# Row numbers and gathers of experts 1 and 2 moved ahead of the first expert's products in a mixture-of-experts decoder step

## What is computed

```python
logits = x @ w_router + b_router
top_v, top_e = lax.top_k(logits, 4)
gates = jax.nn.softmax(top_v, axis=-1)
# for each expert e, over the rows of the tokens that chose it:
h = xb @ w_gate_up[e] + b_gate_up[e]
gate = jnp.minimum(h[:, 0::2], 7.0)
up = jnp.clip(h[:, 1::2], -7.0, 7.0)
out = ((up + 1.0) * gate * jax.nn.sigmoid(gate * 1.702)) @ w_down[e] + b_down[e]
# y = h_in + sum over the four chosen experts of gate * out, then RMSNorm
```

## Time and profile before

| | us |
|---|---|
| median of three runs | 1385.93 |
| the profiled execution | 1385.96 |
| its span, first to last instruction | 1384.1 |
| TensorE busy (matmul) | 1352.9 |
| VectorE busy | 1209.8 |
| ScalarE busy | 1091.7 |
| GpSimd busy | 1010.1 |
| weights moved, with all else | 458.99 MB, mean 332 GB/s |

### The profile page before, as it was taken

One profiled execution on the slowest core, in us unless ns is written; L12 is line 12 of the kernel. 1 busy time (PEld: TensorE's weight loads), 2 busy tenths in 40 slices (PEclk: granted clock), 3 DMA queues, 4 the chain that ended last, 5 costly groups with the idle time before them and its releaser, 6 DMA issues.

```text
span 1384.1 us, 19701 instructions
## 1 busy us (share of the span) xinstructions
PE 1352.9 (98%) x6762; PEld 994.0 (72%) x6762; DVE 1209.8 (87%) x1092; ACT 1091.7 (79%) x1149; POOL 1010.1 (73%) x431
## 2 busy tenths in 40 slices
PE   8999999999999999999999999999999999999995
PEld 5988655667777777777777777777777777777773
DVE  5466556899999999999999999999999999999996
ACT  5354423778888888888888888888888888888885
POOL 2122211266699999899999998999999989999943
PEclk9999999999999999999999999999999999999998
DMA  9522272999999999999999999999999999999984
GB/s 354 189 66 72 88 276 70 367 394 356 372 351 377 378 369 382 372 392 379 377 393 373 378 382 375 379 384 365 389 380 365 381 390 374 382 371 386 375 313 150
DMA packets 51803, 458.99 MB, mean 332 GB/s; under 512 B 11450, under 2 KB 15516, under 8 KB 26122
## 3 DMA queue, kind: packets, MB, share of 16 engines
q1 hardware_dynamic: 40089, 438.33, 80.9%
q0 software_dynamic: 10000, 18.19, 6.0%
q10 hardware_dynamic: 1648, 1.65, 0.4%
HBM read 446.62 MB, written 22.08 MB: 339 GB/s over the span
## 4 chain that ended last, share of the span: by engine, by line
PE 77%; DMA 3%; DVE 1%; issue 1%; POOL 1%; ACT 0%; POOLq 0%; ACTq 0%; DVEq 0%
PE psum L2371 24%; PE psum L2373 24%; PE psum L2372 24%; DMA area<-hn_tbl,idx_i 3%; PE psum L2355 2%; PE psum L2366 2%; POOL small L810 0%; DVE low L1690 0%; PE psum L2342 0%; DVE area L1812 0%; POOL area L695 0%; DVE area L1772 0%; DVE ring L1836 0%; DVE area L1765 0%; POOL out L820 0%
## 5 line engine op out<-in xcount | busy, mean ns | idle before, releaser
L1690 DVE TENSOR_TENSOR low<-raw,high 128x2048 fp32r<-128x2048 f32 x384 | 875.1, 2310 | 35.9 <-ACT high L1098 35.8
L1098 ACT CAST high<-raw 128x2048 fp32r<-128x2048 f32 x384 | 727.8, 1913 | 23.7 <-PE psum L2373 19.2
L2371 PE MATMUL psum<-high,area_r 128*104 128x512 f32 x1536 | 610.4, 397 | 2.5 <-DVE area_r L1754 1.4
L2373 PE MATMUL psum<-low,area_r 128*104 128x512 f32 x1536 | 604.3, 393 | 0.0
L2372 PE MATMUL psum<-high,area_r 128*104 128x512 f32 x1536 | 603.9, 393 | 0.0
L668 POOL PARTITION_BROADCAST brow<-brow x192 | 382.8, 2074 | 41.1 <-DMA brow<-in_biases 40.6
L2373 PEld LDWEIGHTS psum<-low,area_r 128*104 128x104 f32 x1536 | 258.0, 168 | 96.5
L2371 PEld LDWEIGHTS psum<-high,area_r 128*104 128x104 f32 x1536 | 258.0, 168 | 95.0 <-DVE area_r L1754 1.6
L2372 PEld LDWEIGHTS psum<-high,area_r 128*104 128x104 f32 x1536 | 258.3, 168 | 90.7
L737 POOL DMA_INDIRECT area<-hn_tbl,idx_i x32 | 162.9, 5089 | 79.5 <-DVE idx_i L1657 40.8
L665 POOL COPY arrived<-cst 1x1 f32 x60 | 199.5, 3325 | 0.3
(11 more groups left out here) (269 smaller groups left out, 1175.5 us busy)
## 6 DMA issues: line engine op xcount, KB each, us to landing
raw<-in_w_gate_up SPq DMA_DIRECT2D x128, 2048.0 KB, 11.1
raw<-in_w_down SPq DMA_DIRECT2D x64, 2048.0 KB, 11.7
ring<-in_w_in SPq DMA_DIRECT2D x7, 1024.0 KB, 15.3
ring<-in_x_prompt SPq DMA_DIRECT2D x8, 512.0 KB, 9.7
ring<-in_w_out SPq DMA_DIRECT2D x7, 512.0 KB, 4.6
ring<-in_w_mem_kv SPq DMA_DIRECT2D x2, 1024.0 KB, 9.3
ring<-in_mem_kT SPq DMA_DIRECT2D x1, 2048.0 KB, 8.5
ring<-in_cache_mem_v SPq DMA_DIRECT2D x1, 2048.0 KB, 8.2
```

Source lines behind the costliest of these rows:

```text
L1098: nc.scalar.copy(high_w(i), raw_w(t)).then_inc(sem("w_high"), 1)
L1690: v.tensor_tensor(low_w(t), raw_w(t), high_w(i), ALU.subtract).then_inc(sem("w_low"), 1)
L2371: mm(bank, high, wh, start=False, stop=False, skip_group_check=True)
L2373: return mm(bank, high, wl, start=False, stop=stop, skip_group_check=True)
```

## The change

It moves work and waits; the number of products of the experts stays.

- GpSimd loads the zero register ahead of the waits for `hn_tbl`. In the head it waits for gather 0, then issues `gather(1, 1)`, then `gather(2, 2)`. Period 0 makes no gather any more. The gathers of even and odd experts count on two semaphores.
- VectorE copies `cnt` before the last gates, and runs `hot_slots(1, 1)` ahead of its flag load. In the head: `slot_info(0)`, `slot_info(1)`, `low_part` 10, `x_low(0)`, `low_part` 11 and 12, `hot_slots(2, 0)`, `low_part` 13, `slot_info(2, 2)`. Period 0 has no `hot_slots` and `slot_info`; within a period `swiglu` and `act_low` stand ahead of the table work of the same step.
- TensorE no longer loads the flag before the first expert, but after the loop over the middle experts; its eight spare products there are gone. In the head it runs `info(1, 1)`, 14 spare products into bank 4, `x_rows(0)`, 10 more spares, the first two half-chunks, and `info(2, 0)`. The transposes of expert 0 wait for two gate columns instead of one.
- SyncE issues chunks 3 to 5 after the first half of `x_rows(0)` (`xg_pe`) instead of on the landing of gather 0.

```diff
@@ sync
-            sp.wait_ge(sem("gathered"), 16)
+            sp.wait_ge(sem("xg_pe"), 1)
             sp.wait_ge(sem("group_pe"), 2)
@@ gpsimd
-            for par, n in ((0, 3), (1, 2)):
-                pool.wait_ge(sem(f"st_hn{par}"), 16 * n)
-
             bound = pool.alloc_register("bound")
             pool.wait_ge(sem("eid_zero"), 1)
             none = pool.value_load(eid_i[0:1, EXTRA:EXTRA + 1], min_val=0, max_val=0)
+            for par, n in ((0, 3), (1, 2)):
+                pool.wait_ge(sem(f"st_hn{par}"), 16 * n)
...
-                    bounds_check=bound, oob_is_err=False).then_inc(sem("gathered"), 16)
+                    bounds_check=bound, oob_is_err=False).then_inc(sem(f"gathered{k % 2}"), 16)
...
                 wait(pool, "w_used", (m - 1) * HALVES + 9)
+                if not m:
+                    pool.wait_ge(sem("gathered0"), 16)
                 gather(m + 1, 1)
                 if not m:
+                    gather(2, 2)
                     bias_rows(1, 0)
 
             def period(n, k, last=False, table=False, bare=False, overflow=False):
-                old = not (last or table or bare)
+                old = not (last or table or bare) and not (isinstance(n, int) and n == 0)
...
-                if old and not overflow or table:
+                if old and not overflow or table or isinstance(n, int) and n == 0:
                     bias_rows(n + 2, 0)
@@ vector
             v.tensor_scalar(idx_i[0:CAP, 0:1], banks[6][0:CAP, 416:417], float(NT), None, ALU.add).then_inc(sem("idx_ready"), 1)
+            link(v.tensor_copy(cnt, banks[0][:, 160:192]))
             gates(NTT - 1, NTT, NSM, 3)
...
-            link(v.tensor_copy(cnt, banks[0][:, 160:192]))
...
             link(v.tensor_copy(flag_i[:, :], wk[:, 9, 1:2]))
+            hot_slots(1, 1)
             flag = dv.value_load(flag_i[0:1, 0:1], min_val=0, max_val=1)
...
                     slot_info(0, 0, again=False)
+                    slot_info(1, 1)
                     low_part(m - 1, 10, True)
-                else:
-                    hot_slots(m, 0)
-                    slot_info(m, 0)
+                    x_low(0)
+                    low_part(m - 1, 11, True)
+                    low_part(m - 1, 12, True)
+                    hot_slots(2, 0)
+                    low_part(m - 1, 13, True)
+                    slot_info(2, 2)
+                    return
...
-                old = not (last or table or bare)
+                old = not (last or table or bare) and not (isinstance(n, int) and n == 0)
...
+                    if i == 2:
+                        swiglu(n, 0)
+                    if i == 4:
+                        act_low(n, 0)
+                    if i == 6:
+                        swiglu(n, 1)
                     if isinstance(n, int) and n == 0 and i == 4:
                         table_keys()
...
-                    if i == 2:
-                        swiglu(n, 0)
-                    if i == 4:
-                        act_low(n, 0)
-                    if i == 6:
-                        swiglu(n, 1)
@@ tensor
-            def spare(count, bank, tile):
+            def spare(count, bank, tile, start=True):
 
                 for _ in range(count):
-                    mm(bank[:, 0:P], tile, tile, start=True, stop=True)
+                    mm(bank[:, 0:P], tile, tile, start=start, stop=True, skip_group_check=True)
...
-                pe.wait_ge(sem("gathered"), n * 16 + 16)
+                pe.wait_ge(sem(f"gathered{k % 2}"), n * 8 + (8 if k % 2 else 16))
                 if isinstance(n, int) and n in (0, NE):
-                    pe.wait_ge(sem("gcol_ready"), counted(n) + 1)
+                    pe.wait_ge(sem("gcol_ready"), counted(n) + (1 if n else 2))
...
                 if m:
                     info(m, 0)
+                else:
+                    info(1, 1)
+                    spare(14, banks[4], ident, False)
                 x_rows(m, 0)
+                if not m:
+                    spare(10, banks[4], ident, False)
                 pe.wait_ge(sem("x_low"), m * 2 + 2)
                 gate_up(m - 1, 10, True, 0)
                 gate_up(m - 1, 11, True, 0)
-                info(m + 1, 1)
+                if m:
+                    info(m + 1, 1)
+                else:
+                    info(2, 0)
...
-                    if not (table or bare):
+                    if not (table or bare or isinstance(n, int) and n == 0):
                         info(n + 2, k)
...
-            spare(8, banks[1], ident)
-            pe.wait_ge(sem("route_ready"), 1)
-            flag = pe.value_load(flag_i[0:1, 0:1], min_val=0, max_val=1)
             for q in range(6):
...
                     period(it * UB + u, u, table=True)
+            pe.wait_ge(sem("route_ready"), 1)
+            flag = pe.value_load(flag_i[0:1, 0:1], min_val=0, max_val=1)
             for u in range(UB):
```

More of the change, by code:

```diff
@@ L1782, in head @@
                     slot_info(0, 0, again=False)
+                    slot_info(1, 1)
                     low_part(m - 1, 10, True)
-                else:
-                    hot_slots(m, 0)
-                    slot_info(m, 0)
+                    x_low(0)
[5 more added lines that the diff above has]
+                    return
+                hot_slots(m, 0)
+                slot_info(m, 0)
                 hot_slots(m + 1, 1)
                 x_low(m)
-                if not m:
-                    low_part(m - 1, 11, True)
                 low_part(m - 1, 12, True)
@@ L1892, in _ @@
                         period(it * UB + (NE + u), u)
-                dv.wait_ge(sem("gathered"), (NE + EXTRA + 2) * 16)
+                for par in range(2):
+                    dv.wait_ge(sem(f"gathered{par}"), (NE + EXTRA + 2) * 8)
                 row_means(2, 2)
@@ L2363, in act_rows @@
                 elif fh == 0:
-                    pe.wait_ge(sem("gcol_ready"), min(n + 2, FROM_TABLE) if isinstance(n, int) else FROM_TABLE)
+                    pe.wait_ge(sem("gcol_ready"), min(max(n + 2, 3), FROM_TABLE) if isinstance(n, int) else FROM_TABLE)
                 for q in range(4):
```

## The result

The changed kernel takes 1389.19 us in the median (1387.93 to 1390.53), beside 1385.90 us for the kernel before in the same comparison. The ratio is 1.0023, with a 95% interval of 1.0017 to 1.0029: 3.3 us slower, where 1386.4 us was forecast and 1388.6 was the end of the range. By the bound of 0.3% this is still "within", but it lies clearly on the slow side, where rival B stood. The profiled execution took 1390.14 us, with a span of 1388.3 (1385.96 and 1384.1 before).

What follows compares the result with a forecast made beforehand. VectorE was taken to bound the kernel up to expert 2, with TensorE following by 0.05 us. VectorE entering expert 1 0.4 us later carried to the end: 1385.96 + 0.4 = 1386.4 us, range 1383.5 to 1388.6.

Steps and rivals of the forecast that it cites:

- rival B: Expert 1's chunk 0 falls behind both gathers: free to 270.7, then one for one; at 273.3, 2.6 us, 1388.6; chance 0.10.
- TensorE's sum: TensorE's gains through expert 2's transposes: 1.0 + 0.8 + 0.4 + 3.0 = 5.2 us, not expected to decide the time.
- new waits for low parts late in expert 0: Sign of being right: TensorE newly waits for low parts or `act_low` late in expert 0, some 1.5 us.
- the cast of chunk 0 released by DMA: Sign of being right: ScalarE's cast of expert 1's chunk 0 is released by its DMA landing, near 271 us.
- A: Rival: TensorE decides, so all 5.2 us of its gains count, 1380.8 us; chance 0.08.
- 1.0 for the clock: TensorE in expert 0: the clock holds, so the products before expert 1's row numbers end 1.0 us earlier.
- 3.0 for the gather stall: TensorE before expert 2's transposes at 310.73: the wait goes, as gather 2 leaves at about 255; 3.0 us.
- the chunk lands 0.5 + 0.7 = 1.2 us later, with 0 and 2.0 as ends: Expert 1's chunk 0: 0.5 us from later issue of chunks 3 to 5, 0.7 from gather 1; lands near 271.1.
- The end of 1.0: Upper end of gather 1's delay to the weights: sharing from the first packet, 0.43 MB at 429 GB/s, 1.0 us.
- The forecast's own lower end: Forecast less 0.8 us for an unchanged chunk landing and 1.5 us for fewer slowdowns of VectorE by GpSimd.
- its own work bounds it: VectorE entering expert 1: if the chunk's landing is unchanged, only its own work limits it, 0.8 us earlier.
- Question G: Asked after the result: is TensorE's own gain of some 5 us hidden behind VectorE, or not there at all?.

Runs made afterwards that it cites:

- the order repair alone: Changed kernel with chunk 0 of expert 1 issued ahead of chunk 5 of expert 0: 1387.63 us, ratio 1.0008.
- the run with both repairs: Changed kernel with expert 1's chunk 0 issued ahead of expert 0's chunk 5, and gather 2 issued in period 0: 1387.91 us, ratio 1.0018.

## Why the prediction was wrong

**What held.** VectorE decides up to expert 2, with a lead of 0.06 us, and TensorE's sum doesn't reach the end. No gather stall, the full clock through the head, new waits for low parts late in expert 0 (2.85 us, forecast some 1.5), and the cast of chunk 0 released by DMA: each came as said. From that cast to the low part it took 3.92 us, forecast 4.02. A fell. Of TensorE's 5.2 us two terms rest on one execution: 1.0 for the clock and 3.0 for the gather stall, neither of which shows in every profiled run that keeps that part of the kernel before.

**The step that failed** is the term "the chunk lands 0.5 + 0.7 = 1.2 us later, with 0 and 2.0 as ends". It landed 4.4 us later. In its parts:

- The issue of chunks 3 to 5: 1.60 us later (246.10 against 244.50), forecast 0.5. Of this 0.86 had come in ahead of the change's work (row numbers of expert 0 at 237.72 against 236.86): this execution ran at half the clock for a while at 233 us. The change's own part is 0.74. Gather 0 left 1.50 us after its numbers (239.38 against 237.88), where 0.93 was taken.
- The gather: I charged its bytes at the rate of the weights, 1.0 us at most, and took 0.7. It costs 2.8 us (issue to cast 28.2 us instead of 25.4). I also had gather 1 meet only the beginning of the weights, and it ran in their midst. It even moves less than I took: the trace has 75 packets of 4 KB for expert 0, 73 for expert 1 and 92 for expert 2, not 104. The stretch up to chunk 0's cast held 68 of them before (those of gather 1) and 165 after, 97 more: 0.40 MB, 0.9 us by bytes. The trace before had the row to see it in. The table gives 429 GB/s from 247.5 us but 404 in the stretch from 265, into which gather 1 falls, and smaller windows on the trace before show it plainly. The DMA queues from 258 to 262 us, then from 266 to 270, kernel before (packets, MB, share of 16 engines):

```profile
q1 hardware_dynamic: 121, 1.72, 100.5%
```

```profile
q1 hardware_dynamic: 90, 1.16, 85.7%
q0 software_dynamic: 86, 0.18, 14.1%
```

In 4 us the weights (q1) lose 0.56 MB while the gather (q0) moves 0.18 MB: three bytes of weights for each of its own. By that 0.40 MB displace 1.2 MB, which is 2.8 us at 430 GB/s, as measured; the extra gathers of 73 and 75 rows, 0.31 MB, measured 2.4 and 2.9. "The end of 1.0" was thus no upper end, and I had named a rule with it: The Trainium skill (DMA: Bandwidth & Descriptors, SWDGE vs HWDGE vs iDMA) has each engine go round-robin between the kinds of queues. The direction agrees, the size by bytes does not. No row shows the turns; the rows above show that the weights, with 85.7% of the engines' time, moved 67% of the bytes that they had moved with all of it (1.16 of 1.72 MB), so their packets took longer while the gather ran.

**Rival B's price** was right. It said: free up to 270.7, from there one for one. At 274.3 this gives 3.6 us, 1389.6; the profiled execution took 1390.14, and 0.86 us of its late cast are that execution's own. "I find little more than 2 us of delay" is what kept B at 0.10 and the range's end at 1388.6. With the gather at 2.8 and the issue at 0.7 the chunk lands at 273.4, and B would have been the forecast, 1388.7, against 1389.19 measured. The forecast's own lower end doesn't add up: an unmoved landing is 0.8 us earlier than before and so 1.2, not 0.8, below the forecast.

**What stays open.** Why the changed kernel stays slower once the landing is repaired: the order repair alone gave 1.0008 and not the 0.8 us gain that "its own work bounds it" asked for. The profiled execution of that run had half the clock from 233.9 for 13.7 us, and its first product came 4.9 us later than in the trace before and 3.3 later than in the changed kernel's; whether its median holds a part of this can't be told from one profile. Question G is answered in part: with 14 and 10 spares no pair of runs that differ in the change shows a gain whose intervals part, with 5 and 3 two do. Fewer spare products seem worth 2.6 us (ratios 1.0008 and 0.9989), more than the 1 to 1.5 expected; they were never tried alone. Nor was TensorE's flag load: it cost nothing visible, as the delay in this trace stays at 3.75 us from expert 6 to the last one's transposes.

## What to carry to other kernels

A small transfer moved into a saturated stretch is to be priced by what the main stream loses while one like it is under way, read in narrow windows of the trace, not by its bytes; and then ask which single transfer behind it carries the end. A stall or a drop of the clock read from one execution is to be looked for in a second one before it is counted as a gain. When a follower's stall is removed, first look for the engine that it had been waiting in the shadow of, and lighten that one in the same step. Work moved out of a tight period has to pass every queue that waits for its result: SyncE's wait for the table cost 18 us, and one row more per period on GpSimd cost 4.

## What the runs showed of the hardware

- A gather of 73 or 75 rows of 4 KB put in beside the weight transfers took 2.4 and 2.9 us from them, and the 97 rows more of the changed kernel 2.8: 3 to 4 times what their bytes would.
- Two gathers on GpSimd's queue landed one after the other: the second, issued 5.4 us behind the first, landed 8.0 us behind it and met only the later chunks.
- The granted clock of the head differed between executions with the same gaps: 0.50 for 3.4 us from 247.5 in the trace before, 1.00 with gaps of 0.84, 1.17 and 1.36 us in a run with the same head.
- GpSimd took 1.07 to 1.39 us to issue a gather where VectorE was idle or in small operations (239.38, 245.64), and 2.55 to 9.94 us beside low parts (2.55 at 325.90 in the kernel before, 4.57 at 255.72 in the changed one, 9.94 at 287.88 in the kernel before). The Trainium skill (SBUF — State Buffer, SBUF: two separate sides) has a VectorE instruction with two inputs from that memory and a GpSimd operation that reads it lock each other out, whichever starts first. These rows agree.
- It works the other way too. In the run with both repairs VectorE's `table_keys` met a broadcast of GpSimd:

```profile
271.93 0.65 DVE L1670 SCALAR_TENSOR_TENSOR lg<-area,brt 128x160 f32<-128x160 f32 x1
```

and without it, in the changed kernel:

```profile
270.45 0.33 DVE L1668 SCALAR_TENSOR_TENSOR lg<-area,brt 128x160 f32<-128x160 f32 x1
```
